# Evictions that make the stripe order, and conv's u and c as a pair of seven block products

## The reference, cut to what matters

```python
h = rms_norm(x, pre_g)
proj = h @ w_in                       # 12 sections of 1536 columns, 3 of 2048
o_a = dilated_mixture_attn(q_a, k_a, v_a) * silu(z_a)
o_c = b_c * causal_short_conv(c_c * u_c, conv_w, conv_b) * silu(z_c)
o_r = retention(q_r, k_r, v_r) * silu(z_r)         # rotary on q and k, norm of the result
merged = sigmoid(g_a) * (o_a @ w_branch_a) \
       + sigmoid(g_c) * (o_c @ w_branch_c) + sigmoid(g_r) * (o_r @ w_branch_r)
x = x + rms_norm(merged @ w_out, post_g)
```

## Time and profile before

| | |
|---|---|
| median of 3 runs | 2778.6 us (2778.03 to 2779.01) |
| the profiled execution | 2779.1 us |
| span of its records | 2777.1 us |
| mean granted PE clock | 0.999 |
| PE busy | 2757.6 us, 12192 matmuls |
| DVE busy | 1777.7 us |
| ACT busy | 1266.8 us |
| moved by DMA | 579.76 MB, mean 209 GB/s |

### The profile page before, as it was taken

How to read it: one execution, slowest core, us unless ns; L and a number is a source line. 1 busy time by engine, 2 the same in 40 slices (tenths; PEclk the granted TensorE clock), 3 DMA queues, 4 the chain that set the end, 5 groups by cost and what they waited for, 6 DMA issues and landing times.

```text
span 2777.1 us, 30124 instructions
## 1 busy us (share of the span) xinstructions
PE 2757.6 (99%) x12192; PEld 2254.8 (81%) x12192; DVE 1777.7 (64%) x2000; ACT 1266.8 (46%) x1462; POOL 28.1 (1%) x36
## 2 busy tenths in 40 slices
PE   9999999999999999999999999999999999999998
PEld 7888888888888888888878888888888888888887
DVE  6656764555675666578576567645656756666784
ACT  6454543444453334354454545434444533344543
POOL 0000000000000000000000000000000000000000
PEclk9999999999999999999999999999999999999999
DMA  9667465666566676666576674656665656766663
GB/s 333 206 218 227 159 227 190 217 207 212 182 227 197 212 222 202 214 211 214 182 231 201 215 232 152 231 194 212 211 214 180 229 192 202 235 204 213 209 214 121
DMA packets 299291, 579.76 MB, mean 209 GB/s; under 512 B 12304, under 2 KB 37264, under 8 KB 298896
## 3 DMA queue, kind: packets, MB, share of 16 engines
q1 hardware_dynamic: 260976, 517.50, 56.3%
q10 hardware_dynamic: 37168, 55.13, 6.8%
q0 software_dynamic: 1008, 5.20, 0.6%
HBM read 548.43 MB, written 29.36 MB: 208 GB/s over the span
## 4 chain that ended last, share of the span: by engine, by line
PE 94%; DVE 3%; ACT 1%; DMA 1%; issue 0%; POOL 0%; ACTq 0%; DVEq 0%; SPq 0%; POOLq 0%
PE ps L898 30%; PE ps L899 30%; PE ps L900 30%; DVE w_trail L1233 1%; PE ps L852 1%; PE ps L853 1%; PE ps L851 1%; DVE raw L1243 1%; ACT w_lead L972 1%; DMA bounce_z<-z_sb 1%; PE ps L795 0%; PE ps L797 0%; PE ps L794 0%; PE ps L773 0%; PE ps L777 0%
## 5 line engine op out<-in xcount | busy, mean ns | idle before, releaser
L1233 DVE TENSOR_TENSOR w_trail<-raw,w_lead 128x1024 fp32r<-128x1024 f32 x1009 | 1228.0, 1223 | 948.8 <-ACT w_lead L972 945.6
L972 ACT ACTIVATE w_lead<-raw 128x1024 fp32r<-128x1024 f32 x1009 | 1061.9, 1059 | 1375.8 <-PE ps L900 1274.2
L898 PE MATMUL ps<-w_lead,hT_lead 128*128 128x512 f32 x3136 | 1238.7, 395 | 9.6 <-DVE w_trail L1233 6.7
L900 PE MATMUL ps<-w_lead,hT_trail 128*128 128x512 f32 x3136 | 1233.6, 393 | 0.0
L899 PE MATMUL ps<-w_trail,hT_lead 128*128 128x512 f32 x3136 | 1233.5, 393 | 0.0
L898 PEld LDWEIGHTS ps<-w_lead,hT_lead 128*128 128x128 f32 x3136 | 589.2, 188 | 150.2 <-DVE w_trail L1233 11.4
L900 PEld LDWEIGHTS ps<-w_lead,hT_trail 128*128 128x128 f32 x3136 | 589.1, 188 | 135.1
L899 PEld LDWEIGHTS ps<-w_trail,hT_lead 128*128 128x128 f32 x3136 | 589.3, 188 | 132.9
L898 PE MATMUL ps<-w_lead,oT_lead 128*128 128x512 f32 x576 | 224.2, 389 | 0.0
L900 PE MATMUL ps<-w_lead,oT_trail 128*128 128x512 f32 x576 | 224.1, 389 | 0.0
L899 PE MATMUL ps<-w_trail,oT_lead 128*128 128x512 f32 x576 | 224.1, 389 | 0.0
(11 more groups left out here) (125 smaller groups left out, 1048.8 us busy)
## 6 DMA issues: line engine op xcount, KB each, us to landing
raw<-w_in SPq DMA_DIRECT2D x381, 1024.0 KB, 5.2
raw<-w_out SPq DMA_DIRECT2D x32, 1024.0 KB, 5.1
raw<-w_branch_a SPq DMA_DIRECT2D x24, 1024.0 KB, 5.7
raw<-w_branch_c SPq DMA_DIRECT2D x24, 1024.0 KB, 5.2
raw<-w_branch_r SPq DMA_DIRECT2D x24, 1024.0 KB, 5.7
bounce_q<-vq_sb ACTq DMA_DIRECT2D x18, 512.0 KB, 3.3
vq_sb<-bounce_q ACTq DMA_DIRECT2D x72, 128.0 KB, 3.5
bounce_z<-z_sb ACTq DMA_DIRECT2D x18, 512.0 KB, 3.2
```

What stands on the lines that cost most here:

```text
L898: pe.matmul(acc, lead[:, k, tok(t)], wl, start=opens, stop=False)
L900: last = pe.matmul(acc, trail[:, k, tok(t)], wl, start=False, stop=closes)
L972: act.activation(w_lead[:, (l * HALVES + h) % SPLIT_SLOTS, :], raw[:, SLOT_OF[l, i][0], part:part + HALF * COLS], ACT.Copy).then_inc(lead_ ...
L1233: dve.tensor_tensor(w_trail[:, s, :], raw[:, SLOT_OF[l, i][0], part:part + HALF * COLS], w_lead[:, s, :].bitcast(F32), ALU.subtract).then_ ...
```

## The change

`columns()` and `columns_out()` go: PE reads every block straight. The evictions now read PSUM as (h, j, a) and write (j, h, a) (`cut`, `quads`, now with three free dimensions). The rotary tables go back to their natural order, with 64 columns a tile and a table of `neg_sin`; retention's q and k are evicted with as many instructions of as many elements. `x_rstd` moves: the z eviction has none of it any more, attention's row scale and retention's `o_rstd` are multiplied by it (a small multiply on DVE, one on POOL), conv's b is scaled by its square (`x_sq`), and so is the product of u and c.

Conv's blocks come as b, z, u, c, and u and c of every group are a pair as the gates are. Its copies go to `v_sb` and `q_sb`; c's eviction then has a second step that multiplies the two (`conv_joined`). Conv's tables are moved to match.

```diff
-ROLES = {"attention": "vqkz", "conv": "ucbz", "retention": "vqkz"}
+ROLES = {"attention": "vqkz", "conv": "bzuc", "retention": "vqkz"}
...
-PAIRS = [gate_block(m, j) for m in MIXERS for j in PAIRED_GATES[m]]
+PAIRS = sorted([gate_block(m, j) for m in MIXERS for j in PAIRED_GATES[m]]
+               + [first_block("conv", g) + 2 for g in range(GROUPS)])
...
-    "conv": [("prod_away", 2 * B + 1), ("prod_back", 2 * B + 3), ("z_away", 4 * B + 1), ("z_back", 4 * B + 3),
-             ("out", 4 * B + 6)],
+    "conv": [("z_away", 2 * B + 1), ("z_back", 2 * B + 3), ("prod_away", 4 * B), ("prod_back", 4 * B + 2),
+             ("out", 5 * B)],
...
-    "conv": [("prod", 2 * B + 6), ("conv0", 2 * B + 6), ("conv1", 2 * B + 7), ("conv2", 3 * B),
-             ("gate", 4 * B), ("z", 4 * B + 6), ("product", 4 * B + 6), ("out", 4 * B + 7)],
+    "conv": [("gate", 2 * B), ("z", 2 * B + 6), ("prod", 4 * B + 5), ("conv0", 4 * B + 5), ("conv1", 4 * B + 6),
+             ("conv2", 4 * B + 7), ("product", 5 * B), ("out", 5 * B + 1)],
...
+        def pair_tile(n, i, t):
+            kind, _mixer, _role, j = BLOCKS[n][3]
+            if kind == "gate":
+                return gates[:, t, COLS * (j + i):COLS * (j + i + 1)]
+            return quads((v_sb, q_sb)[i], t)
...
         def cut(ap):
-            return ap.rearrange("p (j c) -> p j c", j=QUADS)
+            return ap.rearrange("p (h j a) -> p j h a", h=HPB, j=QUADS)
...
-                pool.tensor_scalar(x_neg, x_rstd, -1.0, 0.0, ALU.mult, ALU.add).then_inc(x_rstd_ready, 1)
+                pool.tensor_tensor(x_sq, x_rstd, x_rstd, ALU.mult).then_inc(x_rstd_ready, 1)
...
-                    rstd(o_ssq, o_mean, l * GROUPS + (g + 1), o_rstd, P, 8).then_inc(o_rstd_ready, 1)
+                    rstd(o_ssq, o_mean, l * GROUPS + (g + 1), o_rstd, P, 8).then_inc(o_pow, 1)
+                    pool.wait_ge(o_pow, l * GROUPS + (g + 1))
+                    by_tile = o_rstd.rearrange("p (h t) -> p h t", t=TILES)
+                    pool.tensor_tensor(by_tile, by_tile, x_rstd.unsqueeze(1).to_broadcast((P, HPB, TILES)),
+                                       ALU.mult).then_inc(o_rstd_ready, 1)
...
-                    wl = columns(n, w_lead[:, slot, i * COLS:(i + 1) * COLS])
-                    wt = columns(n, w_trail[:, slot, i * COLS:(i + 1) * COLS])
+                    wl = w_lead[:, slot, i * COLS:(i + 1) * COLS]
+                    wt = w_trail[:, slot, i * COLS:(i + 1) * COLS]
...
                     for t in range(TILES):
                         dve.wait_ge(*sig_tiles(l, TILES * group_no[mixer, j] + t + 1))
-                        dve.scalar_tensor_tensor(quads(z_sb, t), cut(bank(n, t)[:, :]), x_rstd[:, t:t + 1],
-                                                 quads(z_sb, t), ALU.mult, ALU.mult).then_inc(evicted[n % 2], 1)
+                        dve.tensor_tensor(quads(z_sb, t), cut(bank(n, t)[:, :]), quads(z_sb, t),
+                                          ALU.mult).then_inc(evicted[n % 2], 1)
...
-                elif kind == "mix" and role == "c":
-                    dve.wait_ge(*moved_out(l, n - 1))
-                    dve.wait_ge(*done_block(l, n))
-                    for t in range(TILES):
-                        dve.scalar_tensor_tensor(quads(q_sb, t), cut(bank(n, t)[:, :]), x_rstd[:, t:t + 1],
-                                                 quads(v_sb, t), ALU.mult, ALU.mult).then_inc(evicted[n % 2], 1)
...
+                    if role == "c":
+                        dve.wait_ge(*moved_out(l, n - 1))
+                        dve.wait_ge(*moved_out(l, n))
+                        for t in range(TILES):
+                            dve.scalar_tensor_tensor(quads(q_sb, t), quads(v_sb, t), x_sq[:, t:t + 1], quads(q_sb, t),
+                                                     ALU.mult, ALU.mult).then_inc(conv_joined, 1)
```

More of the change, by code:

```diff
@@ L105, in first_block @@
     return MIXER_BLOCKS * MIXERS.index(mixer) + PER_BLOCK_GROUP * g
-PAIRS = [gate_block(m, j) for m in MIXERS for j in PAIRED_GATES[m]]
+PAIRS = sorted([gate_block(m, j) for m in MIXERS for j in PAIRED_GATES[m]]
+               + [first_block("conv", g) + 2 for g in range(GROUPS)])
+GATE_PAIRS = [n for n in PAIRS if BLOCKS[n][3][0] == "gate"]
 PAIR_OF = {n + i: n for n in PAIRS for i in range(2)}
@@ L313 @@
 VALUES_LATE = 4
-for _n in [first_block("attention", g) for g in range(1, GROUPS)] + [first_block("conv", 0)]:
+for _n in [first_block("attention", g) for g in range(1, GROUPS)]:
     EVICT_DUE[LAST_HALF[_n] + AHEAD + VALUES_LATE] = EVICT_DUE.pop(LAST_HALF[_n] + AHEAD)
@@ L980, in evict @@
                     copy_to = {("attention", "v"): v_sb, ("attention", "q"): q_sb, ("attention", "k"): k_sb,
-                               ("conv", "u"): v_sb, ("conv", "b"): k_sb}.get((mixer, role))
+                               ("conv", "b"): k_sb}.get((mixer, role))
                     if copy_to is not None:
                         act.wait_ge(*done_block(l, n))
-                        before = {("attention", "v"): j - 1, ("conv", "u"): GROUPS - 1 if j == 0 else -1}.get((mixer, role), -1)
+                        before = {("attention", "v"): j - 1}.get((mixer, role), -1)
                         if before >= 0:
@@ L1018, in pair_copy @@
             def pair_copy(l, what, n):
-                mixer, j = BLOCKS[n][3][1], BLOCKS[n][3][3]
-                t, col = {"p1": (0, j), "p6": (0, j + 1), "p7": (1, j)}[what]
+                kind, mixer, _role, j = BLOCKS[n][3]
+                i, t = {"p1": (0, 0), "p6": (1, 0), "p7": (0, 1)}[what]
                 act.wait_ge(*done_product(l, what, n))
-                if what == "p1" and MIXERS.index(mixer) == 1:
-                    for i in range(2):
-                        act.wait_ge(*moved_out(l, branch_block(MIXERS[0], j + i)))
+                if what == "p1" and kind == "mix" and j == 0:
+                    act.wait_ge(*step_ready(l, STEP["values", "attention", GROUPS - 1, HPB // 2 - 1]))
+                elif what == "p1" and kind == "mix":
+                    act.wait_ge(*turned(l, "prod", mixer, j - 1))
+                elif what == "p1" and MIXERS.index(mixer) == 1:
+                    for before in range(j, j + 2):
+                        act.wait_ge(*moved_out(l, branch_block(MIXERS[0], before)))
                 elif what == "p1" and mixer == MIXERS[0] and j == 0 and l > 0:
@@ L1028, in pair_copy @@
                     act.wait_ge(*merged_tiles(l, TILES * (j + 2)))
-                dst = gates[:, t, COLS * col:COLS * (col + 1)]
                 step = STEP["pair", "p1", n]
-                copied = act.activation(dst, side(l, step)[:, :], ACT.Copy)
+                copied = act.activation(pair_tile(n, i, t), in_order(n, side(l, step)[:, :]), ACT.Copy)
                 if what == "p7":
@@ L1064, in send_away @@
                     act.wait_ge(*rotated_tiles(l, TILES * (2 * g + "qk".index(what) + 1)))
+                elif what == "prod":
+                    act.wait_ge(conv_joined, l * (TILES * GROUPS) + TILES * (g + 1))
                 else:
@@ L1245, in pair_rest_of @@
             def pair_rest_of(l, what, n):
-                j, p_step, q_step = BLOCKS[n][3][3], STEP["pair", "p1", n], STEP["pair", "q5", n]
-                t, col = {"p6": (0, j + 1), "p7": (1, j)}[what]
+                p_step, q_step = STEP["pair", "p1", n], STEP["pair", "q5", n]
+                i, t = {"p6": (1, 0), "p7": (0, 1)}[what]
                 if what == "p6":
@@ L1345, in evict @@
                     if gate in PAIR_OF:
-                        dve.wait_ge(gate_ready, TILES * (2 * pair_no(l, PAIR_OF[gate]) + gate - PAIR_OF[gate] + 1))
+                        dve.wait_ge(*gate_sigmoids(l, gate))
                     else:
```

77 lines of the change are left out of this document (40 added, 37 removed).

## The result

The changed kernel takes 2733.74 us (median of 4 runs, 2733.36 to 2734.01) against 2778.81 us of the kernel before, run beside it (2778.03 to 2779.41): a ratio of 0.9838, 95% interval 0.9821 to 0.9855. That is 45.1 us less where 39.2 were forecast. The profiled span went from 2777.1 to 2731.5 us.

What follows compares the result with a forecast made beforehand. PE was taken as the bound, busy 2757.6 of 2777.1 us: matmul count times step, plus stops. 30.7 + 9.3 - 0.8 = 39.2 us off 2778.6 gave 2739.4, said as 2739.5; range 2731 to 2750.

Steps and rivals of the forecast that it cites:

- Part 1: Order moved from PE's reads to the evictions: 48 mixer blocks fall from 22.40 to 21.76 us, gaining 30.7 us.
- Rival C: Chance 0.03: PE's read order did not cost the 6.7 ns a matmul, 48 blocks stay at 22.40 us; 2770 us.
- Part 2: Conv's u and c as a pair: 43.25 us instead of 44.80, gaining 9.3 us in six pairs.
- The stop before unit 5: In each u and c pair, PE waits 1.8 us more than in conv's gate pair for DVE's split 5.
- The second half: Later half of each u and c pair: z's transposes fit into DVE's idle time, 0.1 us taken.
- unit 8: In each u and c pair, PE starts this unit about 0.2 us late, as in conv's gate pair.
- the p6 copy: ACT's copy in each u and c pair, ending at 774.1 where p7 wants it at 774.7: tight, covered.
- Rival A: Chance 0.12: the u and c pair hides its side work in DVE's idle time before unit 5; 2728 us.
- Rival B: Chance 0.20: u and c pairs give nothing back, with a further stop of 1 to 2 us; 2748.7 us.
- Part 3: An added POOL multiply before retention's gate delays its gate pair by 0.4 us in each layer: -0.8 us.
- Rival D: Chance 0.02: ACT stands in `z_back` before split 10 in each conv pair, 6.7 us more on PE; 2779.5 us.

Runs made afterwards that it cites:

- e1: Changed kernel with the pairs of u and c taken out and conv's blocks again in the order u, c, b, z: 2739.8 us, ratio 0.9858.
- e5: Changed kernel with branch blocks' moving operand read, or PSUM written, in runs of various lengths, output columns permuted: 2774.6 us, single execution.
- e2: Changed kernel with conv's gate multiplies moved one unit later, behind the split of the pair's unit 5: 2740.4 us.
- e3: Changed kernel with conv's z eviction, gate multiplies, DRAM trip and transposes of z moved later, behind the pair's tight places: 2742.3 us.

## Why the prediction was right, and where its sizes were off

**The bound** was read rightly: 12120 matmuls and fewer stops explain the whole span.

**Part 1** (30.7 us): measured 30.4 outside the first 96 matmuls and 0.3 in them. The rule of the Trainium skill's page SBUF — State Buffer (Door 1, the note on cachelines), by which two hits or more on a 16-byte line give full bandwidth, does not hold for this read: 39 us in e1, and in e5 268 ns against 226.7 for runs of exactly one such line. Rival C is refuted. The Trainium skill's page PSUM — Partial Sum Buffer (Specifications (TRN2)) says that a non-contiguous PSUM pattern slows matmuls significantly; e5 shows no cost at all for writes in runs down to two words, so on this form it does not hold. DVE and ACT pay nothing for runs of 32.

**Part 2** (9.3 us): measured 12.5, by terms that were mis-sized, not by another mechanism. The stop before unit 5 was put at 1.8 us over conv's gate pair and is 1.43. The working charged each pair of DVE operations with its full 1.29 to 1.37 us, but the next operation starts 1.20 us after the first of them did (483.26, 484.46; 487.92, 489.12), so split 5 ended 0.3 us earlier than drawn. The second half cost nothing instead of 0.1, and unit 8 a little less than in the gate pair. In all a pair is 0.54 us shorter than forecast, six are 3.2. The rest was as described: unit 8 late by 0.15 (0.2), `z_back` with 1.76 us of issues, the p6 copy through at 498.34, 0.6 us before p7. That margin was real: e2 used it up. The working took the trip of `z_away` at its median of 3.2 us; it was 2.9 here and 5.9 in e2, so this margin is smaller than it looks. Rival A (0.12) is refuted, the stop is there. Rival B did not come about in the changed kernel, but its mechanism, a wait in `z_back`, is in part what made e2 slower and what cost e3 its gain.

**Part 3** (-0.8 us): wrong in sign, +1.3. The multiply costs what was said: DVE waits 1.81 us for POOL in group 2 where it waited 1.53. The step that failed is the next: that a delay of 0.3 us would pass down a trip to DRAM unchanged. The trip from issue to landing took 7.1 us before and 6.5 after, and its way back 2.67 and 1.81 us of issues; beside the gain load its length varies from run to run by more than the multiply costs (6.5 to 7.5 us for the trip, 41.8 to 43.7 for the pair). The gain here lies within that scatter: it is luck of one profile, not of the change.

**Outside the sum**: 0.7 us in the first 96 matmuls, beyond the 0.3 of part 1: PE waits there for the first loads. They took 24.9 us before, 23.9 in the changed kernel and 23.3 to 24.4 in the other kernels that share this start, so I count it as scatter, not as a gain. Part 3's error of 2.1 us, this, the pairs' 3.2 and 0.4 of small change add up to the 6.4 us by which the profiled span beat the forecast; the medians beat it by 5.9.

**DVE and ACT**: forecast 1900 and 1305 us busy, measured 1890.0 and 1304.1. Of DVE's difference the z evictions' dropped scalar, which the forecast of 1900 left out, is 2.2 us (25.3 to 23.1); the overlap just named, 0.08 us for each of some 16 operations more in a pair, would give most of the rest. **Rival D** (ACT stuck in `z_back`) is refuted for the changed kernel and shown as possible by e3: 5.4 us, once `z_away` went out among chunk loads.

## What to carry to other kernels

Where an engine feeds the bound one with no slack over a stretch, it is the place of its other work that costs, not the amount: read which split stands behind each step, and move the step, with all its DMAs, behind the last tight one. A wait for a DMA on an in-order queue is to be placed where the work behind it has lead, as far from its issue as the buffers allow, since a trip's length depends on what else is being loaded: the same half megabyte took 2.9 us when the next load was issued a microsecond after it, 5.9 when it was issued a microsecond before (e2), and 5.6 to 7.3 among three loads (e3); the order of trip and load was not varied by itself. A small move of a step can change which comes first. And a re-ordering that some engine must do is best put on the one that isn't the bound and that pays nothing for it.

## What the runs showed of the hardware that was not expected

- The order in which PE reads its moving operand in fp32r costs from 3 ns less to 261 ns more than the straight read for a matmul of 512 columns (223.6 to 487 ns a step), and not by run length alone: runs of 4 words cost 268 ns a step with hops of 512 bytes and 223.6 with hops of 64, which is less than the 226.7 of the straight read.
- Writing PSUM in runs of 32, 8 or 2 words cost a matmul nothing (226.7 ns).
- In these pairs most DVE operations start 0.08 us before the record of the one before has ended (a split of 1.23 us at 482.12, the next operation at 483.26), so a chain is shorter than the sum of its durations. A chunk sum behind a split does not: it starts 0.03 us after the split's end (484.46 + 1.22, 485.71).
- In e3's second layer PE stopped for 2.0 to 3.2 us before unit 17 in each of the three pairs. After it two to five steps were of the ordinary length, and then some seven to nine matmuls went at 427 ns a step instead of 227: the granted clock had fallen from 2.4 to 1.2 GHz. Its mean is the number before the last two here, 0.76 over the 7 us around the first of these stops. In the first layer stops of 1.8, 2.4 and 0.65 us at the same place left the clock as it was. The length of the stop alone does not tell the two apart (2.4 us left it, 2.0 us did not), and what does is not shown.

```profile
1872.00:1879.00 7.00, 5.47 (x17) 4.35 (x18) 5.82 (x6) 3.89 (x5) 0.00 (x0) 0.76 0.68 230
```
